# One gather of 8 KB rows for the u and v row of an expert, each pair handled on its own

## The chip, the cores and the metric

One Trainium2 chip; the kernel runs on one of its cores. The metric is the device time of one execution in microseconds (us). The median of three runs of the kernel before is 3246.3 us (3240.91 to 3247.57).

## The reference

Two transformer-like blocks of two layers each, on 256 tokens of width 1024, all in float32. The part that the change touches is the mixture of experts at the end of both layers of the second block. For each token it picks the 128 best of 16384 experts (8 heads with 16 each), with a gate for each. Every expert has a row `u` and a row `v` of 1024 numbers. The result is

```
act = einsum('td,thkd->thk', x, u_tab[idx])        # one dot product per picked expert
wgt = gelu(act) * gate
y   = einsum('thk,thkd->td', wgt, v_tab[idx])      # the weighted sum of the v rows
```

## The kernel before

The kernel is one program of many stages, one after the other on the core. Each stage is a block in which the five engines run their own instruction streams and meet at semaphores.

The experts are computed in two ways side by side. For 192 of the 256 tokens (`DENSE`) all 16384 experts are computed as matrix products, with gates that are zero where an expert was not picked. There are 128 rows of 128 experts (`NK`). For the other 64 tokens (`ROWS_OF`) only the picked experts are used: 64 tokens by 128 picks are 8192 pairs of token and expert, laid on 128 partitions by 64 columns, so that two partitions share a token. For each of the 64 columns an indirect DMA fetches one `u` row per partition, later another fetches one `v` row per partition, 4 KB per partition, 512 KB in all.

`experts_stage` (from line 2637, run from 1729 to about 2285 us and from 2666 us to the end) does both. Its parts:

- SyncE (SP) fetches the matrix tiles: `v` tiles of 512 KB into a ring of four (line 255), `u` tiles of 512 KB (line 2683) into another ring of four.
- PE takes, for each row j of experts, ten matmuls of 128x512 (`combine`, lines 2731 to 2735) and, for all rows from the 35th on, the `u` products of a row two further on (`activate`, line 2718). The first 28 rows (`EARLY`) have had their `u` product in an earlier stage, six more (`MID`) too.
- ACT splits each `v` tile in two float32r parts: it writes the high one (`high`, line 2784), and applies gelu to the `u` products (line 2777).
- DVE writes the low part (`low`, line 2844), weighs the activations with the gates (`weigh`, lines 2834, 2836, 2815), and between these does the work of the 64 other tokens: `dot` (line 2851) multiplies a gathered `u` row with the token and sums it into a column of `row_act`; `add_row` (lines 2859 and 2862) adds a gathered `v` row times its weight to `y_rows`.
- POOL issues the 128 gathers (line 2708) into a ring of six slots of 4 KB (`row_ring`, `ROW_SLOTS`), first all `u` rows, then all `v` rows. Gather n waits until the row that lay in its slot has been used: `pool.wait_ge(row_step, n - ROW_SLOTS + 1)`.

The order is written out by hand: `order` (line 2647) is a list of 228 steps, a v step (`low` of a tile two rows ahead) and a u step (`weigh` of a row two ahead) in turn once the early rows are over. DVE and ACT walk through it in the same order. `dots_at` and `adds_at` (line 2656) say after which steps a dot or an add is put. All 64 dots come at steps 3 to 124, all adds at steps 131 to 227. Between them stands one gelu over all 64 columns on ACT (line 2795) and one multiplication by the gates on DVE (line 2879). DVE may run ahead of PE by two rows at most, since the split ring has two places (`SPLIT`) and the weights two buffers. PE in turn can take a row only when its weights and both its halves are there (`weighted`, `low_ready`).

The same 24 KB per partition that hold the six slots are also the place where the stage before keeps the six `u` tiles of the `MID` rows (line 2304). `y_rows` holds two thirds of their activations until they are weighed. `choose_stage` writes the indices of the rows into `row_at` (line 2519).

Of the kernel before, what the change touches and what calls it, by code (L numbers as in the profile page):

```python
# [72 lines left out]
EARLY = 28  # L73
# [2 lines left out]
DENSE = 192  # L76
ROWS_OF = SEQ - DENSE
PEER = NK * NK
ROW_SLOTS, MID = 6, 6

RAW, SPLIT = 4, 2
SUMS_LATE = 3
# [2183 lines left out]
def choose_stage(k, l, weights, norm, ahead):  # L2266
# [3 lines left out]
    nc, pairs = k.nc, TB * PH  # L2270
# [3 lines left out]
    with stage(nc, *WEIGHT_SEMS, "keys_in", "kept", "scored", "scores_used", "row_step", "step", "gate_step", "turned",  # L2274
# [136 lines left out]
        def _(dve):  # L2411
# [21 lines left out]
            rows = Steps(dve, row_step)  # L2433
# [5 lines left out]
            s = Steps(dve, step)  # L2439
# [73 lines left out]
            own, at, rows = slice(SLOTS, 2 * SLOTS), k.late_at[:, 0:SLOTS], slice(DENSE - P, P)  # L2513
            s(nc.vector.scalar_tensor_tensor(at, k.key_i[:, own], float(NK), k.key_j[:, own], ALU.mult, ALU.add))
            dve.wait_ge(gate_step, 6)
            for half in range(2):
                to, cols = slice(half * ROWS_OF, (half + 1) * ROWS_OF), slice(half * ROWS_OF, (half + 1) * ROWS_OF)
                for which in range(2):
                    nc.vector.tensor_scalar(k.row_at[to, which, :], at[rows, cols], float((2 * l + which) * PEER), None, ALU.add).then_inc(step, 1)
                nc.vector.tensor_copy(k.row_gate[to, :], k.gates[rows, SLOTS + half * ROWS_OF:SLOTS + (half + 1) * ROWS_OF]).then_inc(step, 1)  # L2520
            dve.wait_ge(turned, 1)
            for n, x in enumerate((k.slot_i, k.slot_j, k.slot_gate)):
# [114 lines left out]
def experts_stage(k, l, weights, norm, ahead, out_dram):  # L2637
# [4 lines left out]
    nc, rows = k.nc, NK - EARLY  # L2642
# [9 lines left out]


    sums = ROWS_OF
    places = sorted([*range(3, EARLY, 4), *(t for t in range(EARLY + 2 * MID, len(order)) if is_v[t]), *range(EARLY + 2 * MID + 1, len(order) - 8, 6)])
    dots_at, adds_at = places[:sums], places[-sums:]
    gelu_at, weigh_at = dots_at[-1] + 1, dots_at[-1] + 2
    assert weigh_at < adds_at[0], (weigh_at, adds_at[0])
    row_slot = lambda n: k.row_ring[:, n % ROW_SLOTS, :]
    rows_there = lambda n: 16 * (l * len(range(n % ROW_SLOTS, 2 * sums, ROW_SLOTS)) + n // ROW_SLOTS + 1)  # L2660

    with stage(nc, *WEIGHT_SEMS, "u_in_0", "u_in_1", "u_in_2", "u_in_3", "u_done", "gelu_done", "weight_step", "weighted", "kept_0", "kept_1", "turned", "added", "stored", "ahead_high", "ahead_low",
               "row_step", "row_gelu", "row_weighed", *Norm.SUMS, weights=weights) as (
            block, high_ready, low_ready, halves_used, u_in_0, u_in_1, u_in_2, u_in_3, u_done, gelu_done, weight_step, weighted, kept_0, kept_1, turned, added, stored, ahead_high, ahead_low,
            row_step, row_gelu, row_weighed, squared, sums_done):
        weights.signals(high_ready, low_ready, halves_used)
        u_in = (u_in_0, u_in_1, u_in_2, u_in_3)
        if norm:
# [32 lines left out]

        @block.gpsimd
        def _(pool):
            for n in range(2 * sums):
                if n >= ROW_SLOTS:
                    pool.wait_ge(row_step, n - ROW_SLOTS + 1)
                at = k.row_at[:, n // sums, n % sums:n % sums + 1]
                nc.gpsimd.indirect_dma_start(row_slot(n), None, k.peer_rows, bass.IndirectOffsetOnAxis(ap=at, axis=0)).then_inc(  # L2708
                    k.rows_in[n % ROW_SLOTS], 16)

        @block.tensor
        def _(pe):
# [43 lines left out]
                late_row((rows - MID) // RAW, m)  # L2756
            for j in range(NK - 2, NK):
                combine(j, j % 2, False, j == NK - 1)
            pe.wait_ge(row_step, 2 * sums)
            for m in range(pairs):  # L2760
                pe.wait_ge(kept_0, m // 2 + 1)
                pe.wait_ge(kept_1, m // 2 + 1)
                for c in (2 * m, 2 * m + 1):
                    out, cols = k.ps[:, turned_in[m], c % 2 * SEQ:(c % 2 + 1) * SEQ], slice(c * P, (c + 1) * P)
# [7 lines left out]
        @block.scalar  # L2772
        def _(act):
            def activate(q):
                act.wait_ge(u_done, q - MID + 1)
                act.wait_ge(weighted, q + EARLY + 1)
                nc.scalar.activation(k.gelu[:, q % 2, 0:DENSE], k.ps[:, q % 2, 0:DENSE], ACT.Gelu_apprx_tanh).then_inc(gelu_done, 1)  # L2777

            def high(j):

                act.wait_ge(weights.loaded[j % RAW], 16 * (j // RAW + 1))
                for half, cols in enumerate(weights.halves):
                    act.wait_ge(halves_used, v_used(j - SPLIT) + half - 1)
                    nc.scalar.activation(weights.split[:, weights.half_slot(j), 0, cols], weights.ring[:, weights.slot(j), cols], ACT.Copy).then_inc(high_ready, 1)  # L2784

            act.sem_inc(gelu_done, 2)
            weights.high_given(act)
            for t, (v, n) in enumerate(order):
                if v and n + SPLIT < NK:
                    high(n + SPLIT)  # L2790
                if not v and n >= MID:
                    activate(n)
                if t == gelu_at:
                    act.wait_ge(row_step, sums)
                    nc.scalar.activation(k.row_act[:, :], k.row_act[:, :], ACT.Gelu_apprx_tanh).then_inc(row_gelu, 1)
            if norm:
                ahead.high_ahead(act, 0, weights.left(NK - 2))
            act.wait_ge(halves_used, v_used(NK - 1))
            for half in range(2):
                nc.scalar.activation(k.y_natural[:, 0, half * 512:(half + 1) * 512], outs[half], ACT.Copy).then_inc(kept_0, 1)  # L2800
            if norm:
                norm.warm(act)
            for m in range(pairs if norm else 0):
                act.wait_ge(added, m + 1)
                nc.scalar.activation(norm.squares[:, 2 * m:2 * m + 2, :], k.x2T[:, 2 * m:2 * m + 2, :], ACT.Square).then_inc(squared, 2)
            if norm:
                ahead.high_ahead(act, 1, weights.left(NK - 1))

        @block.vector
        def _(dve):  # L2810
# [36 lines left out]
            def dot(n):  # L2847


                dve.wait_ge(k.rows_in[n % ROW_SLOTS], rows_there(n))  # L2850
                nc.vector.tensor_tensor_reduce(row_slot(n), row_slot(n), k.x_rows, 1.0, 0.0, ALU.mult, ALU.add,  # L2851
                                               k.row_act[:, n:n + 1]).then_inc(row_step, 1)

            def add_row(n):
                w = k.row_weight[:, n - sums:n - sums + 1]
                dve.wait_ge(k.rows_in[n % ROW_SLOTS], rows_there(n))
                if n == sums:
                    dve.wait_ge(row_weighed, 1)
# [9 lines left out]
            for t, (v, n) in enumerate(order):  # L2868
                if v and n + SPLIT < NK:
                    low(n + SPLIT)  # L2870
                if t + SPLIT < EARLY:
                    split_early(t + SPLIT)
                if not v:
                    weigh(n)
                for n in [n for n, at in enumerate(dots_at) if at == t]:
                    dot(n)
                if t == weigh_at:
                    dve.wait_ge(row_gelu, 1)
                    nc.vector.tensor_tensor(k.row_weight[:, :], k.row_act[:, :], k.row_gate[:, :], ALU.mult).then_inc(row_weighed, 1)
                for n in [n for n, at in enumerate(adds_at) if at == t]:  # L2880
                    add_row(sums + n)
            if norm:
                ahead.low_ahead(dve, 0, 0)
            dve.wait_ge(halves_used, v_used(NK - 1))
# [10 lines left out]
def second_block(k, scope, sb, out):  # L2895

    nc = k.nc
# [8 lines left out]
    k.hot_i, k.hot_j = hot(16, NK), hot(16, NK)  # L2906
    gates = sb(scope, "gates", SEQ * NK)
    k.pair, k.h2F = sb(scope, "pair", ROWS_OF), sb(scope, "h2F", DC, SEQ)
    k.row_at = sb(scope, "row_at", 2, ROWS_OF, dtype=U32)
    k.row_gate, k.row_act, k.row_weight = (sb(scope, f"row_{n}", ROWS_OF) for n in ("gate", "act", "weight"))  # L2910
    tail = Carver(gates[:, DENSE * NK:])
    k.early = gates[:, 0:EARLY * DENSE].rearrange("p (j t) -> p j t", j=EARLY)
    k.dense = gates[:, EARLY * DENSE:DENSE * NK]
    k.u_ring = gates[:, 0:RAW * D].rearrange("p (s m) -> p s m", s=RAW)
    k.x_rows, k.y_rows, k.row_ring = tail(D), tail(D), tail(ROW_SLOTS, D)


    mix = Carver(gates)
# [44 lines left out]
def layout2(x):  # L2963
# [23 lines left out]
    return {  # L2987
        "small2_dram": small2, "w_mixing": mixing.reshape(L * MIX_TILES, P, D), "w_choose": np.concatenate([query, pu[:, :EARLY]], axis=1).reshape(-1, P, D),
        "peer_keys": x["peer_keys"].transpose(0, 4, 1, 2, 3).reshape(L, P, HC * NK),
        "peer_u": pu[:, EARLY:].reshape(-1, P, D), "peer_v": pv.reshape(-1, P, D), "peer_rows": np.stack([x["peer_u"], x["peer_v"]], axis=1).reshape(-1, D),  # L2990
    }


# [229 lines left out]
```

## Time and profile before

| what | us |
|---|---|
| median of three runs | 3246.3 |
| profiled execution, its own time | 3233.7 |
| its span, first to last instruction | 3231.9 |
| first experts stage, from its first gather to its last add | 1730 to 2285 |
| second experts stage | 2666 to 3232 |

Busy time of an engine is the time in which it worked on an instruction, waiting left out; a busy share near 1 in a stretch says that this engine sets its pace. The columns of a windows view are: stretch, its length, busy us of PE, of its weight loads (PEld), of DVE, ACT and POOL, each with the number of instructions, then the granted clock of TensorE (1.00 is 2.4 GHz, 0.50 is 1.2 GHz), the mean busy share of the 16 DMA engines and the GB/s that they moved. In a timeline, times in square brackets are idle time before the instruction, with what ended it.

### The profile page before, as it was taken

How to read it: one execution, taken by the hardware profiler on the slowest of the kernel's cores; microseconds unless marked ns; L12 is line 12 of the kernel's file. 1: busy time of each engine (PE TensorE's matmuls, PEld its weight loads, DVE VectorE, ACT ScalarE, POOL GpSimd, SP SyncE). 2: the span in 40 equal slices, each digit the busy share in tenths (PEclk: the TensorE clock that was granted, in tenths of full speed). 3: DMA queues.
4: the chain of work that ended last, by engine and by line, in shares of the span. 5: the costliest groups of instructions: out<-in, count | busy, mean ns of one | idle time of the engine just before them, and what ended most of it. 6: DMA issues, size and time to landing. Idle time of an engine off the chain costs nothing. (4 is left out here: it accounts for less than half of the span.)

```text
span 3231.9 us, 52114 instructions
## 1 busy us (share of the span) xinstructions
PE 3097.7 (96%) x17744; PEld 2679.3 (83%) x17744; DVE 2371.6 (73%) x4997; ACT 1403.3 (43%) x2729; POOL 632.0 (20%) x556
## 2 busy tenths in 40 slices
PE   7899999999999999899999999999999998999999
PEld 5767776777867999888987799999789986899998
DVE  5667776776666677565978788788656887887887
ACT  5454333332336665475356333333465274333332
POOL 0000000000000000064434132222356061222221
PEclk9999999999999999899999999999999999999999
DMA  6115533434322545433545799999434518899996
GB/s 222 43 59 183 176 144 113 154 124 158 110 71 87 174 156 168 148 121 115 170 130 210 274 354 356 328 356 356 159 101 140 183 50 318 313 353 339 343 357 249
DMA packets 176414, 643.50 MB, mean 199 GB/s; under 512 B 20352, under 2 KB 20736, under 8 KB 175360
## 3 DMA queue, kind: packets, MB, share of 16 engines
q1 hardware_dynamic: 138672, 504.62, 45.0%
q0 software_dynamic: 36864, 134.23, 11.3%
q10 hardware_dynamic: 720, 2.71, 0.2%
q8 instruction: 78, 1.28, 0.2%
q14 instruction: 80, 0.66, 0.1%
HBM read 640.44 MB, written 1.05 MB: 198 GB/s over the span
## 5 line engine op out<-in xcount | busy, mean ns | idle before, releaser
L338 ACT ACTIVATE split<-ring 128x512 fp32r<-128x512 f32 (+1 forms) x644 | 397.6, 624 | 699.4 <-PE ps L224 666.5
L224 PE MATMUL ps<-hT,split 128*128 128x512 f32 (+1 forms) x3504 | 631.1, 341 | 6.5 <-DVEq L322 3.4
L224 PEld LDWEIGHTS ps<-hT,split 128*128 128x128 f32 x3504 | 546.5, 191 | 91.3 <-DVE hT L593 9.7
L347 POOL TENSOR_TENSOR split<-ring,split 128x512 fp32r<-128x512 f32 x184 | 244.3, 1338 | 1528.3 <-ACT split L338 1523.7
L2718 PE MATMUL ps<-h2F,gates 128*128 128x192 f32 x3008 | 519.2, 326 | 0.0
L347 DVE TENSOR_TENSOR split<-ring,split 128x512 fp32r<-128x512 f32 (+1 forms) x460 | 307.2, 678 | 283.3 <-ACT split L338 282.4
L2718 PEld LDWEIGHTS ps<-h2F,gates 128*128 128x128 f32 x3008 | 498.4, 190 | 17.1
L2784 ACT ACTIVATE split<-ring 128x512 fp32r<-128x512 f32 x504 | 317.4, 632 | 358.3 <-PE ps L2735 333.6
L2844 DVE TENSOR_TENSOR split<-ring,split 128x512 fp32r<-128x512 f32 x504 | 340.1, 689 | 118.0 <-ACT split L2784 115.4
L2708 POOL DMA_INDIRECT gates<-peer_rows,row_at x256 | 267.7, 1046 | 809.9 <-DVE row_act L2851 462.9
L2731 PE MATMUL ps<-split,chunk 128*128 128x512 f32 x512 | 232.1, 453 | 16.9 <-DVE chunk L2815 16.3
L2777 ACT ACTIVATE gelu<-ps 128x192 f32<-128x192 f32 x188 | 62.1, 330 | 370.2 <-PE ps L2718 370.2
L224 PE MATMUL ps<-h2T,split 128*128 128x256 f32 x1632 | 209.1, 285 | 4.3 <-DVE gates L2147 3.5
L224 PEld LDWEIGHTS ps<-h2T,split 128*128 128x128 f32 x1632 | 199.1, 191 | 11.8 <-DVE h2T L591 5.4
L2733 PE MATMUL ps<-split,chunk 128*128 128x512 f32 x512 | 203.6, 398 | 0.0
L2734 PE MATMUL ps<-split,chunk 128*128 128x512 f32 x512 | 203.4, 397 | 0.0
L2735 PE MATMUL ps<-split,chunk 128*128 128x512 f32 x512 | 203.2, 397 | 0.0
L2732 PE MATMUL ps<-split,chunk 128*128 128x512 f32 x512 | 202.7, 396 | 0.0
L224 PE MATMUL ps<-act_chunk,split 128*128 128x512 f32 (+1 forms) x1056 | 191.9, 343 | 0.0
L224 PEld LDWEIGHTS ps<-act_chunk,split 128*128 128x128 f32 x1056 | 164.2, 192 | 25.0 <-issue 0.6
L2862 DVE SCALAR_TENSOR_TENSOR gates<-gates,row_weight 128x1024 f32<-128x1024 f32 x126 | 161.0, 1278 | 0.2
L2851 DVE CUSTOM_DVE_ANT_0 gates<-gates 128x1024 f32<-128x1024 f32 x128 | 155.9, 1218 | 0.0
(394 smaller groups left out, 4758.2 us busy)
## 6 DMA issues: line engine op xcount, KB each, us to landing
ring<-peer_v SPq DMA_DIRECT2D x256, 512.0 KB
gates<-peer_u SPq DMA_DIRECT2D x200, 512.0 KB, 6.9
ring<-w_up SPq DMA_DIRECT2D x88, 512.0 KB, 3.8
ring<-w_choose SPq DMA_DIRECT2D x88, 512.0 KB, 3.5
ring<-w_mixing SPq DMA_DIRECT2D x68, 512.0 KB, 3.6
ring<-w_merge SPq DMA_DIRECT2D x64, 512.0 KB, 4.1
ring<-w_down SPq DMA_DIRECT2D x44, 512.0 KB, 3.7
mix_row_ring<-w_mod SPq DMA_DIRECT2D x40, 512.0 KB, 3.7
```

The source lines that it names most:

```text
L224: ins = nc.tensor.matmul(out, lhsT(a), rhs(b), start=first and n == 0, stop=last and n == len(PASSES) - 1)
L338: self.nc.scalar.activation(self.split[:, self.half_slot(s), 0, cols], self.ring[:, self.slot(s), cols], ACT.Copy).then_inc(self.high_read ...
L347: (ops or self.nc.vector).tensor_tensor(self.split[:, self.half_slot(s), 1, cols], self.ring[:, self.slot(s), cols], self.split[:, self.ha ...
L2708: nc.gpsimd.indirect_dma_start(row_slot(n), None, k.peer_rows, bass.IndirectOffsetOnAxis(ap=at, axis=0)).then_inc(k.rows_in[n % ROW_SLOTS] ...
L2718: last = nc.tensor.matmul(k.ps[:, m % 2, 0:DENSE], k.u_ring[:, m % RAW, c * P:(c + 1) * P], k.h2F[:, c, 0:DENSE], start=c == 0, stop=c == ...
L2731: nc.tensor.matmul(outs[half], high, v(0), start=first, stop=False)
L2732: nc.tensor.matmul(outs[2 + half], pair, v(0), start=first, stop=False)
L2733: nc.tensor.matmul(outs[half], low, v(0), start=False, stop=False)
L2734: nc.tensor.matmul(outs[2 + half], pair, v(1), start=False, stop=last)
L2735: ins = nc.tensor.matmul(outs[half], high, v(1), start=False, stop=last)
L2784: nc.scalar.activation(weights.split[:, weights.half_slot(j), 0, cols], weights.ring[:, weights.slot(j), cols], ACT.Copy).then_inc(high_re ...
L2844: nc.vector.tensor_tensor(weights.split[:, weights.half_slot(j), 1, cols], weights.ring[:, weights.slot(j), cols], weights.split[:, weight ...
```

## The change

The table of rows in memory is laid out anew: the `u` and `v` row of an expert lie side by side in one row of 8 KB. One gather fetches both. The ring has three slots of 8 KB in the same place. The column n of picks is then dotted, activated, weighed and added for itself. The gather of column n + 3 waits for the add of column n. Gelu and the multiplication with the gate are done on ACT, on one column of 128x1, at the step after each dot. New lists say when: the first three dots at steps 3, 11 and 19, the first add at step 40, then an add and a dot in turn, each at the next of the listed places.

```diff
-ROW_SLOTS, MID = 6, 6
+ROW_SLOTS, MID = 3, 6
...
-                for which in range(2):
-                    nc.vector.tensor_scalar(k.row_at[to, which, :], at[rows, cols], float((2 * l + which) * PEER), None, ALU.add).then_inc(step, 1)
+                nc.vector.tensor_scalar(k.row_at[to, :], at[rows, cols], float(l * PEER), None, ALU.add).then_inc(step, 1)
...
-    places = sorted([*range(3, EARLY, 4), *(t for t in range(EARLY + 2 * MID, len(order)) if is_v[t]), *range(EARLY + 2 * MID + 1, len(order) - 8, 6)])
-    dots_at, adds_at = places[:sums], places[-sums:]
-    gelu_at, weigh_at = dots_at[-1] + 1, dots_at[-1] + 2
+    places = sorted([*range(3, EARLY, 4), *(t for t in range(EARLY + 2 * MID, len(order)) if is_v[t]), *range(EARLY + 2 * MID + 1, len(order) - 8, 4)])
+    places = [*places[:2 * ROW_SLOTS:2], *[t for t in places if t > order.index((False, MID - 1))]]
+    places = [places[n * len(places) // (2 * sums)] for n in range(2 * sums)]
+    dots_at = [*places[:ROW_SLOTS], *places[ROW_SLOTS + 1:2 * sums - 1:2]][:sums]
+    adds_at = [*places[ROW_SLOTS:2 * sums - ROW_SLOTS:2], *places[2 * sums - ROW_SLOTS:2 * sums]]
+    adds_at = adds_at[-sums:]
+    gelu_at = {at + 1: n for n, at in enumerate(dots_at)}
...
-            for n in range(2 * sums):
+            for n in range(sums):
                 if n >= ROW_SLOTS:
-                    pool.wait_ge(row_step, n - ROW_SLOTS + 1)
-                at = k.row_at[:, n // sums, n % sums:n % sums + 1]
-                nc.gpsimd.indirect_dma_start(row_slot(n), None, k.peer_rows, bass.IndirectOffsetOnAxis(ap=at, axis=0)).then_inc(
+                    pool.wait_ge(row_added, n - ROW_SLOTS + 1)
+                at = k.row_at[:, n:n + 1]
+                nc.gpsimd.indirect_dma_start(pair_of(n), None, k.peer_rows, bass.IndirectOffsetOnAxis(ap=at, axis=0)).then_inc(
...
+            def weigh_row(n):
+                w = k.row_weight[:, n:n + 1]
+                act.wait_ge(row_step, n + 1)
+                nc.scalar.activation(w, k.row_act[:, n:n + 1], ACT.Gelu_apprx_tanh).then_inc(row_gelu, 1)
+                act.wait_ge(row_gelu, n + 1)
+                nc.scalar.activation(w, w, ACT.Copy, scale=k.row_gate[:, n:n + 1]).then_inc(row_weighed, 1)
...
-                if t == gelu_at:
-                    act.wait_ge(row_step, sums)
-                    nc.scalar.activation(k.row_act[:, :], k.row_act[:, :], ACT.Gelu_apprx_tanh).then_inc(row_gelu, 1)
+                if t in gelu_at:
+                    weigh_row(gelu_at[t])
...
             def add_row(n):
-                w = k.row_weight[:, n - sums:n - sums + 1]
-                dve.wait_ge(k.rows_in[n % ROW_SLOTS], rows_there(n))
+                w = k.row_weight[:, n:n + 1]
+                dve.wait_ge(row_weighed, n + 1)
...
-                if t == weigh_at:
-                    dve.wait_ge(row_gelu, 1)
-                    nc.vector.tensor_tensor(k.row_weight[:, :], k.row_act[:, :], k.row_gate[:, :], ALU.mult).then_inc(row_weighed, 1)
...
-"peer_rows": np.stack([x["peer_u"], x["peer_v"]], axis=1).reshape(-1, D)
+"peer_rows": np.stack([x["peer_u"], x["peer_v"]], axis=2).reshape(-1, 2 * D)
```

At the end of the stage PE waits for the 64th add (`row_added`) where it waited for the 128th step of `row_step`.

## Rows read from the trace of the kernel before

**Rows 1.** The page: busy us of each engine, and the granted clock in slices.
```profile
PE 3097.7 (96%) x17744; PEld 2679.3 (83%) x17744; DVE 2371.6 (73%) x4997; ACT 1403.3 (43%) x2729; POOL 632.0 (20%) x556
...
PEclk9999999999999999899999999999999999999999
```

**Rows 2.** Windows over the first experts stage (columns as told above).
```profile
1730.00:1820.00 90.00, 81.98 (x327) 61.30 (x327) 71.73 (x180) 39.82 (x64) 14.01 (x13) 0.96 0.85 303
1820.00:2055.00 235.00, 235.00 (x1244) 213.73 (x1243) 188.36 (x405) 76.38 (x144) 61.23 (x58) 1.00 0.93 340
2055.00:2275.00 220.00, 220.00 (x1161) 199.84 (x1160) 184.39 (x328) 71.76 (x135) 58.72 (x57) 1.00 0.94 348
```

**Rows 3.** Waits, 2060 to 2270 us: total us, times, longest.
```profile
POOL gates L2708 <- DVE gates L2862: 143.9, 54, 4.0
...
DVE split L2844 <- ACT split L2784: 17.8, 56, 0.4
DVE gated L2834 <- ACT gelu L2777: 11.9, 29, 0.4
```

**Rows 4.** Timeline of PE: the same matmul in two rows, start and length.
```profile
1936.76 0.53 PE L2731 MATMUL ps<-split,chunk 128*128 128x512 f32 x1
...
1941.68 0.53 PE L2731 MATMUL ps<-split,chunk 128*128 128x512 f32 x1
```

**Rows 5.** Groups by line, 1820 to 2275 us; L2519 by itself.
```profile
L2862 DVE SCALAR_TENSOR_TENSOR gates<-gates,row_weight 128x1024 f32<-128x1024 f32 x59 | 75.4, 1278 | 0.0
L2851 DVE CUSTOM_DVE_ANT_0 gates<-gates 128x1024 f32<-128x1024 f32 x57 | 69.4, 1217 | 0.0
...
L2851 DVE DVE_READ_ACCUMULATOR2_ANT row_act<- 128x1 f32 x57 | 4.6, 81 | 0.0
...
L2879 DVE TENSOR_TENSOR row_weight<-row_act,row_gate 128x64 f32<-128x64 f32 x1 | 0.2, 218 | 0.0
...
L2795 ACT ACTIVATE row_act<-row_act 128x64 f32<-128x64 f32 x1 | 0.2, 249 | 0.0
...
L2519 DVE TENSOR_SCALAR row_at<-gates x8: 186/190/193, 1652.3 to 2589.8; 64x64 uint32<-64x64 f32 x8
```

**Rows 6.** Timeline of DVE, 2156 to 2161 us: lows, add, weighing.
```profile
2156.68 1.28 DVE L2844 TENSOR_TENSOR split<-ring,split 128x512 fp32r<-128x512 f32 x2
2157.88 1.27 DVE L2862 SCALAR_TENSOR_TENSOR gates<-gates,row_weight 128x1024 f32<-128x1024 f32 x1
2159.15 0.51 DVE L2834 TENSOR_TENSOR gated<-gelu,gates 128x192 f32<-128x192 f32 x1
...
2160.67 0.69 DVE L2844 TENSOR_TENSOR split<-ring,split 128x512 fp32r<-128x512 f32 x1 [0.26 <-ACT split L2784]
```

**Rows 7.** DMA issues by line: size, median us from issue to landing.
```profile
gates<-peer_u SPq DMA_DIRECT2D x200, 512.0 KB, 6.9
...
gates<-peer_keys SPq DMA_DIRECT2D x2, 1024.0 KB, 4.8
```

**Rows 8.** The gathers, the last at 3199.1 us, and windows after it.
```profile
L2708 POOL DMA_INDIRECT gates<-peer_rows,row_at x256: 933/1042/1912, 1729.9 to 3199.1; - x128
...
3199.00:3202.00 3.00, 3.00 (x17) 2.68 (x16) 2.25 (x6) 1.26 (x2) 1.04 (x1) 1.00 0.88 322
3202.00:3205.00 3.00, 3.00 (x17) 2.66 (x16) 2.50 (x6) 0.76 (x2) 0.00 (x0) 1.00 0.90 358
3205.00:3208.00 3.00, 3.00 (x20) 2.89 (x18) 2.35 (x3) 0.83 (x2) 0.00 (x0) 1.00 0.07 30
```

**Rows 9.** One window of 1 us at the start of the stage.
```profile
1732.00:1733.00 1.00, 1.00 (x6) 0.82 (x5) 0.00 (x0) 0.45 (x1) 0.69 (x2) 1.00 1.03 422
```

**Rows 10.** PE over its longest gap: timeline, then windows.
```profile
1805.99 0.80 PE L2731 MATMUL ps<-split,chunk 128*128 128x512 f32 x1 [3.75 <-DVE chunk L2815]
...
1803.00:1804.00 1.00, 0.00 (x0) 0.00 (x0) 1.00 (x2) 0.00 (x0) 0.00 (x0) 1.00 0.67 221
1805.00:1811.00 6.00, 5.00 (x12) 3.94 (x13) 2.76 (x9) 0.96 (x2) 0.96 (x1) 0.50 0.53 173
```

More of the change, by code:

```diff
@@ L2654, in experts_stage @@
     sums = ROWS_OF
-    places = sorted([*range(3, EARLY, 4), *(t for t in range(EARLY + 2 * MID, len(order)) if is_v[t]), *range(EARLY + 2 * MID + 1, len(order) - 8, 6)])
-    dots_at, adds_at = places[:sums], places[-sums:]
-    gelu_at, weigh_at = dots_at[-1] + 1, dots_at[-1] + 2
-    assert weigh_at < adds_at[0], (weigh_at, adds_at[0])
-    row_slot = lambda n: k.row_ring[:, n % ROW_SLOTS, :]
-    rows_there = lambda n: 16 * (l * len(range(n % ROW_SLOTS, 2 * sums, ROW_SLOTS)) + n // ROW_SLOTS + 1)
+    places = sorted([*range(3, EARLY, 4), *(t for t in range(EARLY + 2 * MID, len(order)) if is_v[t]), *range(EARLY + 2 * MID + 1, len(order) - 8, 4)])
+    places = [*places[:2 * ROW_SLOTS:2], *[t for t in places if t > order.index((False, MID - 1))]]
+    assert len(places) >= 2 * sums, len(places)
+    places = [places[n * len(places) // (2 * sums)] for n in range(2 * sums)]
[3 more added lines that the diff above has]
+    gelu_at = {at + 1: n for n, at in enumerate(dots_at)}
+    assert len(adds_at) == sums and all(dots_at[n] > adds_at[n - ROW_SLOTS] for n in range(ROW_SLOTS, sums))
+    assert len(gelu_at) == sums
+    pair_of = lambda n: k.pair_ring[:, n % ROW_SLOTS, :]
+    row_slot = lambda n, which: k.pair_ring[:, n % ROW_SLOTS, which * D:(which + 1) * D]
+    rows_there = lambda n: 16 * (l * len(range(n % ROW_SLOTS, sums, ROW_SLOTS)) + n // ROW_SLOTS + 1)
     with stage(nc, *WEIGHT_SEMS, "u_in_0", "u_in_1", "u_in_2", "u_in_3", "u_done", "gelu_done", "weight_step", "weighted", "kept_0", "kept_1", "turned", "added", "stored", "ahead_high", "ahead_low",
-               "row_step", "row_gelu", "row_weighed", *Norm.SUMS, weights=weights) as (
+               "row_step", "row_gelu", "row_weighed", "row_added", *Norm.SUMS, weights=weights) as (
             block, high_ready, low_ready, halves_used, u_in_0, u_in_1, u_in_2, u_in_3, u_done, gelu_done, weight_step, weighted, kept_0, kept_1, turned, added, stored, ahead_high, ahead_low,
-            row_step, row_gelu, row_weighed, squared, sums_done):
+            row_step, row_gelu, row_weighed, row_added, squared, sums_done):
         weights.signals(high_ready, low_ready, halves_used)
@@ L2758, in _ @@
                 combine(j, j % 2, False, j == NK - 1)
-            pe.wait_ge(row_step, 2 * sums)
+            pe.wait_ge(row_added, sums)
             for m in range(pairs):
@@ L2850, in dot @@
                 dve.wait_ge(k.rows_in[n % ROW_SLOTS], rows_there(n))
-                nc.vector.tensor_tensor_reduce(row_slot(n), row_slot(n), k.x_rows, 1.0, 0.0, ALU.mult, ALU.add,
+                u = row_slot(n, 0)
+                nc.vector.tensor_tensor_reduce(u, u, k.x_rows, 1.0, 0.0, ALU.mult, ALU.add,
                                                k.row_act[:, n:n + 1]).then_inc(row_step, 1)
             def add_row(n):
-                w = k.row_weight[:, n - sums:n - sums + 1]
-                dve.wait_ge(k.rows_in[n % ROW_SLOTS], rows_there(n))
-                if n == sums:
-                    dve.wait_ge(row_weighed, 1)
-                    nc.vector.tensor_scalar(k.y_rows, row_slot(n), w, None, ALU.mult).then_inc(row_step, 1)
-                else:
-                    dve.wait_ge(row_step, n)
-                    nc.vector.scalar_tensor_tensor(k.y_rows, row_slot(n), w, k.y_rows, ALU.mult, ALU.add).then_inc(row_step, 1)
+                w = k.row_weight[:, n:n + 1]
+                dve.wait_ge(row_weighed, n + 1)
+                if n == 0:
+                    nc.vector.tensor_scalar(k.y_rows, row_slot(n, 1), w, None, ALU.mult).then_inc(row_added, 1)
+                else:
+                    dve.wait_ge(row_added, n)
+                    nc.vector.scalar_tensor_tensor(k.y_rows, row_slot(n, 1), w, k.y_rows, ALU.mult, ALU.add).then_inc(row_added, 1)
             dve.sem_inc(weighted, 2)
@@ L2876, in _ @@
                     dot(n)
-                if t == weigh_at:
-                    dve.wait_ge(row_gelu, 1)
-                    nc.vector.tensor_tensor(k.row_weight[:, :], k.row_act[:, :], k.row_gate[:, :], ALU.mult).then_inc(row_weighed, 1)
                 for n in [n for n, at in enumerate(adds_at) if at == t]:
-                    add_row(sums + n)
+                    add_row(n)
             if norm:
@@ L2908, in second_block @@
     k.pair, k.h2F = sb(scope, "pair", ROWS_OF), sb(scope, "h2F", DC, SEQ)
-    k.row_at = sb(scope, "row_at", 2, ROWS_OF, dtype=U32)
+    k.row_at = sb(scope, "row_at", ROWS_OF, dtype=U32)
     k.row_gate, k.row_act, k.row_weight = (sb(scope, f"row_{n}", ROWS_OF) for n in ("gate", "act", "weight"))
@@ L2914, in second_block @@
     k.u_ring = gates[:, 0:RAW * D].rearrange("p (s m) -> p s m", s=RAW)
-    k.x_rows, k.y_rows, k.row_ring = tail(D), tail(D), tail(ROW_SLOTS, D)
+    k.x_rows, k.y_rows, k.pair_ring = tail(D), tail(D), tail(ROW_SLOTS, 2 * D)
+    k.row_ring = k.pair_ring.rearrange("p s (n m) -> p (s n) m", n=2)
     mix = Carver(gates)
@@ L2989, in layout2 @@
         "peer_keys": x["peer_keys"].transpose(0, 4, 1, 2, 3).reshape(L, P, HC * NK),
-        "peer_u": pu[:, EARLY:].reshape(-1, P, D), "peer_v": pv.reshape(-1, P, D), "peer_rows": np.stack([x["peer_u"], x["peer_v"]], axis=1).reshape(-1, D),
+        "peer_u": pu[:, EARLY:].reshape(-1, P, D), "peer_v": pv.reshape(-1, P, D), "peer_rows": np.stack([x["peer_u"], x["peer_v"]], axis=2).reshape(-1, 2 * D),
     }
```

## The prediction

> **What bounds the kernel now.** I read the page first, for which engine fills the span. PE is busy 96% of it, DVE 73%, and the granted clock is full almost everywhere [rows 1]. An average over stages does not say what an experts stage waits for, so I cut the first one in windows. From 1820 to 2275 us PE is busy for every microsecond (235.00 of 235, 220.00 of 220), at clock 1.00. DVE stands at 188.4 of 235 and 184.4 of 220, the DMA engines at 0.93 to 0.94 with 340 to 348 GB/s [rows 2]. PE sets the pace; DVE has some 16 to 20% to spare. The waits say the same from the other side: DVE waits for ACT and ACT for PE, in short pieces of at most 0.4 us, and nobody on DVE waits for a gather. Only POOL waits long, for adds to free a slot (143.9 us in 54 waits), which costs nothing there [rows 3]. The timeline gives the price of a row of experts: the same matmul comes again after 1941.68 - 1936.76 = 4.92 us [rows 4]. A row is one v and one u step of the list, so a step takes 2.46 us at PE's pace.
>
> **The change, part by part.** The bytes stay: 64 gathers of 1 MB for 128 of 512 KB. The dots and adds stay too, 64 each per stage. What moves is when a slot comes free. Before, slot n was free after a dot or an add six uses back, so a gather had some nine steps to land. Now the two rows of a pair share a slot, and it is held from the dot until the add, because the gather of pair n + 3 waits for add n. I worked out the two lists from the diff. Add n stands at steps 40, 42, 45, 49 ..., dot n + 3 at steps 41, 44, 46, 50 .... From the first add (40) to dot 63 (220) there are 61 such pairs of places and 180 steps. 90 steps lie between an add and the dot that needs its slot (36 times one step, 21 times two, 4 times three) and 90 between that dot and the next add. The dot-to-add distance is 6 to 8 steps, in which the slot only waits. So the gather is asked to come in 1 to 3 steps, and DVE, which runs in order, stands still at the dot until it lands. Behind the dot queue the low parts and the weighings on which PE's next rows depend.
>
> The **cycle of DVE per pair** is then: gather (G), dot, 1.5 steps, add. With the pieces taken where DVE runs back to back: a dot 1.22 [rows 5], an add 2159.15 - 2157.88 = 1.27, a v step 2157.88 - 2156.68 = 1.20, a u step 2160.67 - 2159.15 - 0.26 = 1.26, so 1.23 for a mean step [rows 6]. That makes 1.22 + 1.5 x 1.23 + 1.27 = 4.3 us beside G. The 1.5 steps after an add run beneath the gather. PE needs 180 / 61 = 2.95 steps x 2.46 = 7.3 us per pair. So DVE becomes the bound as soon as G is over 7.3 - 4.3 = 3.0 us.
>
> **How long is G?** No gather of 1 MB is in the trace, so I bound it. From below: a plain transfer of 1 MB (128 rows of 8 KB) lands 4.8 us after its issue [rows 7], and a gather should not be quicker, since the POOL instruction itself lasts 1.04 [rows 8]. From above: 512 KB tiles fetched in a burst land in 6.9 us [rows 7]; the last gather of 512 KB, issued at 3199.1 with a v tile, a u tile and another gather under way, had DMA traffic behind it until between 3205 and 3208, so 6 to 9 us [rows 8]. At 422 GB/s, the highest rate that the engines show [rows 9], 1.05 MB takes 2.5 of the 4.8 us, which leaves 2.3 us fixed. If the gather got only a third of the 350 GB/s of the full stage, G would be 2.3 + 9.0 = 11.3 us. But a slower stage fetches its tiles more slowly: 1.5 rows of 1.05 MB per cycle of about 11 us are 140 GB/s. Between the steady 350 and the peak of 422 I take 385; 245 are left for the gather, so 1.05 MB takes 4.3 us and G is 6.6 us. That is nearer to the quiet row than to the crowded ones, as the queues are emptier than before.
>
> The Trainium skill has a fit for this path ("DMA: Bandwidth & Descriptors", "Anatomy of one DMA — SWDGE (gpsimd) path"): some 2.0 us plus the bytes at 436 GB/s. Its estimate is 4.4 us for 1 MB against 3.2 for 512 KB, which speaks for one large gather and still leaves DVE waiting; the sum would be about 3440 us by it.
>
> **ACT.** Two activations of 128x1 come after each dot; the nearest row is the 128x64 gelu of 0.249 us [rows 5], so 0.5 us a pair, 32 us a stage on an engine busy a third of it [rows 2]. ACT now waits for the dot, with the high part of the next v tile and the next gelu behind it. The dot is what DVE waits at too, so both are released together; DVE has one step (1.23) of work before it needs ACT again. Between nothing and 0.5 us a pair I take 0.25. The weights themselves are ready 5 steps before the add.
>
> **Small ones.** Four dots fewer stand in the early rows (steps 7 to 27 had six, now two), 4 x 1.22 = 4.9 us of DVE. There PE is busy 82 of 90 us and DVE 72 [rows 2], so part of it shows. The dot at step 27 stood right before the weighing that ended a gap of 3.75 us and a time at clock 0.50 [rows 10]; without it perhaps 3 us more come back. From 0 to 8 us a stage, I take 5. Two of four index writes of 0.19 us go, and one multiplication of 0.22 [rows 5]: under 1 us.
>
> **The sum.** Stretch from add 0 to dot 63 in one stage: 61 x (6.6 + 0.25) + 61 x 1.22 + 60 x 1.27 + 90 x 1.23 = 418 + 74 + 76 + 111 = 679 us. At PE's pace it was 180 x 2.46 = 443. So +236 a stage, +472 in two, less 10 early: +462 on the profiled execution's 3233.7, which gives 3696. That execution lies 12.6 us under the median of the runs (3246.3); with them, 3708, and I say 3705. With G = 4.8 and no ACT term it is 3233.7 + 2 x (293 + 261 - 443) - 16 + 12.6 = 3452; with 11.3, 2 x (705 + 261 - 443) more than before: about 4290.
>
> **The rivals.**
> - Clock. PE would idle some 4 us in each cycle of 11. The one gap of that size now, 3.75 us, is followed by at least 6 us at 0.50, and the matmuls take longer in it [rows 10]. 6 us at half rate cost 3 us of PE work: 7.3 + 3 = 10.3 per pair, just beneath the cycle, so in the forecast it hides. If gelu results come late by it and DVE waits again, a cycle grows by up to 3 us: 122 x 3 = 366 more, 4070; half of it, 3890, is the likelier size. The Trainium skill ("TensorE: Matmul & The Clock Gate", "HAM oscillation — how this bites in real kernels") tells of just this, bursts of matmuls between DMA waits that each start at the low clock.
> - The gather lands near its quiet time, 4.8 to 5.3 us: 3450 to 3520. The rows of 8 KB may move faster than two of 4 KB, and the tiles may be done before each gather starts.
> - Faster. The gather fits in the 3.0 us of cover, PE stays the bound and only the early dots count: 3246 - 10 = 3236. It decides at G = 3.0. Moving the bytes takes 2.5 us even alone [rows 9], and nothing of this size landed under 4.8 [rows 7].
> - Nothing happens: DVE's lead of two rows, 9.8 us, swallows the waits. It would swallow one, not 61 in a row, each of which is 4 us longer than PE's 7.3. Or the lists keep fewer gathers waiting than I read: 3246.
>
> **How the numbers follow.** Forecast 0.70, clock 0.15, near-quiet gather 0.09, faster 0.03, nothing 0.03. The range leaves out the two last, the far half of the clock's case and G over 8.7: 3500 to 3960. Slower by over 0.2% (about what a measurement here tells from no change) 0.94, within 0.03, faster 0.03.
>
> **What would show it.** DVE's longest wait becomes the dot, for the gather, 61 times a stage, about 3 to 5 us each, some 500 us in all; POOL's wait for the add stays. PE idles a third of the stage with DVE as releaser, busy near 65%. DMA falls from 345 GB/s to about 230, in the first 90 us from 303 to about 260. The stage from 1820 us grows by some 235 us. I am wrong if the dots do not wait, if the second wait is ACT's for the dot with DVE's behind ACT, or if the clock stays at 0.50 and DVE waits for gelu.

## The result, and the profile after

The changed kernel takes 3724.2 us (median of six runs, 3711.97 to 3736.59), the kernel before 3249.2 us in the same runs. The ratio is 1.1455, 95% interval 1.1422 to 1.1487: 14.6% slower. The forecast was 3705 us with 3500 to 3960 around it.

The page of the changed kernel, its first parts:

```profile
PE 3254.0 (88%) x17744; PEld 2777.7 (75%) x17744; DVE 2341.8 (63%) x4991; ACT 1424.9 (38%) x2983; POOL 495.2 (13%) x428
...
PEclk9999999999999989999988888889999998898888
...
q0 software_dynamic: 18432, 134.23, 9.7%
```

Against [rows 1] PE fell from 96% to 88% of the span and DVE from 73% to 63%, though neither has less work (DVE 2341.8 us for 2371.6): it is waiting that came in. PE's busy time even grew by 156 us without one matmul more. The clock row says why: it stands at 8 to 9 tenths in the experts stages, so the same matmuls last longer.

Windows over the first experts stage, the same stretches as in [rows 2]:

```profile
1730.00:1820.00 90.00, 82.31 (x339) 61.04 (x338) 69.54 (x180) 42.58 (x74) 3.06 (x3) 1.00 0.78 264
1820.00:2055.00 235.00, 181.90 (x822) 157.74 (x821) 120.60 (x247) 52.77 (x135) 20.38 (x20) 0.86 0.61 226
2055.00:2275.00 220.00, 166.90 (x749) 144.77 (x749) 113.97 (x231) 49.24 (x124) 20.28 (x20) 0.87 0.64 234
```

Where PE was busy 235.00 of 235 us it is now 181.90, and DVE 120.60 for 188.36. The DMA engines fell from 340 to 226 GB/s. No engine is full any more, so a chain of waits sets the pace. The waits of 2060 to 2270 us, to be held against [rows 3], name its links:

```profile
POOL gates L2714 <- DVE gates L2874: 184.6, 18, 11.3
ACT row_weight L2795 <- DVE row_act L2864: 125.5, 19, 9.3
DVE gates L2864 <- DMA gates<-peer_rows,row_at: 101.4, 19, 6.8
...
PE ps L2737 <- DVE chunk L2827: 53.1, 17, 5.9
...
DVE split L2856 <- ACT split L2790: 0.4, 1, 0.4
```

DVE waits for a gather at 19 dots of this stretch, 101.4 us, where before it never did. PE waits for DVE's weights behind it, ACT for the dot, and POOL for the add. DVE itself waits for ACT once, 0.4 us. Over the whole kernel the wait at the dot is 633.5 us in 122 times:

```profile
DVE gates L2864 <- DMA gates<-peer_rows,row_at: 633.5, 122, 8.1
```

122 is 2 x 61, every dot but the first three of each stage. The timeline of DVE shows one cycle:

```profile
2042.36 1.28 DVE L2874 SCALAR_TENSOR_TENSOR gates<-gates,row_weight 128x1024 f32<-128x1024 f32 x1
2043.56 0.50 DVE L2846 TENSOR_TENSOR gated<-gelu,gates 128x192 f32<-128x192 f32 x1
...
2044.39 0.43 DVE L2827 TENSOR_TENSOR chunk<-gated,chunk 128x64 fp32r<-128x64 f32 x2
2050.73 1.23 DVE L2864 CUSTOM_DVE_ANT_0 gates<-gates 128x1024 f32<-128x1024 f32 x1 [5.91 <-DMA gates<-peer_rows,row_at]
...
2055.47 1.28 DVE L2874 SCALAR_TENSOR_TENSOR gates<-gates,row_weight 128x1024 f32<-128x1024 f32 x1
```

The add ends at 2043.64, one weighing follows, then 5.91 us of nothing until the pair is there at 2050.73. From dot to the next add there is no wait. Over all pairs, from the start and end times of these instructions, 7.09 us lie between the end of an add and the start of the dot that needs its slot (6.5 to 7.6 for 8 in 10), 2.95 from that dot's start to the start of the next add, and a cycle is 11.32 us. The stretch from add 0 to dot 63 is 686.9 us in the first stage and 686.5 in the second.

Taken apart by the start times of each row's first matmul, in us, both experts stages:

| | before | after |
|---|---|---|
| rows 0 to 28 | 76.0 + 76.6 | 74.4 + 73.8 |
| rows 28 to 34 | 22.4 + 21.9 | 20.3 + 21.4 |
| rows 34 to 127 | 455.7 + 455.7 | 695.7 + 695.9 |
| all else in the span | 2123.5 | 2128.6 |

The late rows lost 480.2 us, rows 0 to 34 gave back 7.0, and the rest is 5 us, less than what that part differs by from run to run (2118 to 2154 us over all the runs below).

### The profile page after: what moved, and what is told of

The parts are those of the page before. It is cut to its first block and busy times, and to the rows that moved or that the text cites. A ratio compares the mean times of both kernels' runs of the same rounds, so it can differ in the third digit from the quotient of the medians.

```text
span 3710.2 us, 52233 instructions
## 1 busy us (share of the span) xinstructions
PE 3254.0 (88%) x17744; PEld 2777.7 (75%) x17744; DVE 2341.8 (63%) x4991; ACT 1424.9 (38%) x2983; POOL 495.2 (13%) x428
## 3 DMA queue, kind: packets, MB, share of 16 engines
q0 software_dynamic: 18432, 134.23, 9.7%
HBM read 640.44 MB, written 1.05 MB: 173 GB/s over the span
## 5 line engine op out<-in xcount | busy, mean ns | idle before, releaser
L2864 DVE CUSTOM_DVE_ANT_0 gates<-gates 128x1024 f32<-128x1024 f32 x128 | 156.8, 1225 | 633.5 <-DMA gates<-peer_rows,row_at 633.5
L2737 PE MATMUL ps<-split,chunk 128*128 128x512 f32 x512 | 254.8, 498 | 339.5 <-DVE chunk L2827 339.3
L2724 PEld LDWEIGHTS ps<-h2F,gates 128*128 128x128 f32 x3008 | 524.5, 198 | 21.6
L2724 PE MATMUL ps<-h2F,gates 128*128 128x192 f32 x3008 | 539.0, 334 | 0.0
L2737 PEld LDWEIGHTS ps<-split,chunk 128*128 128x128 f32 x512 | 108.8, 213 | 402.9 <-issue 359.0
L2790 ACT ACTIVATE split<-ring 128x512 fp32r<-128x512 f32 x504 | 302.0, 624 | 263.1 <-PE ps L2741 240.1
L2856 DVE TENSOR_TENSOR split<-ring,split 128x512 fp32r<-128x512 f32 x504 | 330.1, 686 | 52.4 <-ACT split L2790 52.2
L2795 ACT ACTIVATE row_weight<-row_act 128x1 f32<-128x1 f32 x128 | 25.9, 203 | 840.1 <-DVE row_act L2864 839.8
L2714 POOL DMA_INDIRECT gates<-peer_rows,row_at x128 | 130.6, 1021 | 1430.8 <-DVE gates L2874 1225.7
L2738 PE MATMUL ps<-split,chunk 128*128 128x512 f32 x512 | 228.2, 446 | 0.0
L2739 PE MATMUL ps<-split,chunk 128*128 128x512 f32 x512 | 228.0, 445 | 0.0
L2740 PE MATMUL ps<-split,chunk 128*128 128x512 f32 x512 | 227.0, 443 | 0.0
L2741 PE MATMUL ps<-split,chunk 128*128 128x512 f32 x512 | 226.2, 442 | 0.0
```

The costliest lines, as they stand in the source:

```text
L2724: last = nc.tensor.matmul(k.ps[:, m % 2, 0:DENSE], k.u_ring[:, m % RAW, c * P:(c + 1) * P], k.h2F[:, c, 0:DENSE], start=c == 0, stop=c == ...
L2737: nc.tensor.matmul(outs[half], high, v(0), start=first, stop=False)
L2738: nc.tensor.matmul(outs[2 + half], pair, v(0), start=first, stop=False)
L2739: nc.tensor.matmul(outs[half], low, v(0), start=False, stop=False)
L2740: nc.tensor.matmul(outs[2 + half], pair, v(1), start=False, stop=last)
L2741: ins = nc.tensor.matmul(outs[half], high, v(1), start=False, stop=last)
```

## The experiments

The theory: a gather of 1 MB stands between an add and the next dot on DVE's in-order path, so each of 61 cycles per stage lasts its latency and 4.2 us of DVE work more. Rivals: PE at its low clock sets the pace; the pair-by-pair work (small activations on ACT, dots and adds in turn) costs; the 8 KB rows move badly.

The runs a1, a2, a3 and c1 leave out work or data and were executed once each; their differences are read inside the traces, from the stretch from add 0 to dot 63 and the late rows, which agree between the two stages of a run within a few us.

### a1 and a2: is PE the bound?

```diff
-                    nc.tensor.matmul(outs[half], low, v(0), start=False, stop=False)
```

a1, on the changed kernel:

> The changed kernel with one of the ten matmuls of combine left out per half row (the product of the low part of the weights), so 8 instead of 10 per row of experts; part of the sum is left out. PE's row falls from 4.92 us by 2 x 0.23 to 4.46 us. Theory (the gather between add and dot stands on DVE's path, PE has room): the stretch from add 0 to dot 63 stays at 687 us a stage, the cycle at 11.3 us, and only the rows outside it gain, so 3724 less 0 to 25. Rival (PE at the low clock sets the pace): 0.46 us at full clock or 0.93 at half over 90 rows and two stages, 80 to 165 us less.

a2, on the kernel before:

> The kernel before with the same matmuls left out; part of the sum is left out. PE sets its pace there, so 94 rows x 0.465 us x 2 stages = 87 us less in the late rows and 0 to 10 in the early ones: 3249 - 87 to 97, some 3155. DVE works about 4.1 us a row, less than 4.46, so PE stays the bound. If DVE or the transfers (344 GB/s already) were the next bound close by, clearly less than 87 would come.

a2 took 3141.4 us, 92 less than the profiled execution before (3233.7). Its late rows went from 455.7 to 412.3 us a stage, 87 us in two, as expected of PE's share. a1 took 3690.8 us, 33 under the changed kernel's median, where 0 to 25 were expected. Its span is 21 us under that of the changed kernel's profiled execution, of which 13 are in rows 0 to 34 and 7 in the later ones; the stretch from add 0 to dot 63 hardly moved (681.9 and 685.5 us for 686.9 and 686.5). Windows of a1 and then of the changed kernel:

```profile
2060.00:2480.00 420.00, 299.75 (x1332) 261.57 (x1333) 221.72 (x450) 93.99 (x243) 39.31 (x38) 0.86 0.64 236
```

```profile
2060.00:2480.00 420.00, 317.23 (x1429) 274.97 (x1427) 216.65 (x438) 92.50 (x237) 38.33 (x37) 0.88 0.63 232
```

PE works 299.75 instead of 317.23 us of the same 420 at about the same clock, and the stretch gets shorter by 5 us at most. The same cut is worth 43 us of late rows per stage where PE is the bound and up to 5 where the gather is. The rival of the clock falls: the low clock is real (0.86 to 0.88 in these windows), but nearly all of its cost lies in time in which PE would wait.

### a3 and c1: what the 7.1 us are made of

```diff
-                nc.gpsimd.indirect_dma_start(pair_of(n), None, k.peer_rows, bass.IndirectOffsetOnAxis(ap=at, axis=0)).then_inc(
+                nc.gpsimd.indirect_dma_start(pair_of(n)[:, 0:D], None, k.peer_rows, bass.IndirectOffsetOnAxis(ap=at, axis=0)).then_inc(
...
-"peer_rows": np.stack([x["peer_u"], x["peer_v"]], axis=2).reshape(-1, 2 * D)
+"peer_rows": x["peer_u"].reshape(-1, D)
```

> The changed kernel, but each gather fetches only the u row (4 KB per partition, 512 KB), the lists and waits stay; the v rows are left out, the adds take what lies there. Theory: of the 7.1 us from the end of an add to the dot, 2.3 are fixed and 4.8 are transfer; half the bytes give some 4.7 to 5.2 us, a cycle of 9.1, and 2 x 61 x 2.1 = 256 us less: about 3465. If nearly all of it were fixed cost of a gather: over 3620. If the clock or ACT set the pace instead of the gather: nearly 3724.

It took 3530.1 us, 194 less. Per pair, 5.53 us were left from add to dot, 1.56 less, not 2.1. So the second 512 KB are worth 1.56 us, 336 GB/s. That alone does not tell what the other 5.53 us are. c1 keeps the gather whole and takes the other traffic away:

```diff
-                sp.dma_start(k.u_ring[:, q % RAW, :], tile(k.peer_u, l * rows + MID + q)).then_inc(u_in[q % RAW], 16)
+                sp.dma_start(k.u_ring[:, q % RAW, 0:64], tile(k.peer_u, l * rows + MID + q)[:, 0:64]).then_inc(u_in[q % RAW], 16)
...
-                weights.fetch(sp, j // RAW, j % RAW)
+                sp.dma_start(weights.ring[:, weights.slot(j % RAW), 0:64], tile(weights.dram, weights.base + j)[:, 0:64]).then_inc(weights.loaded[j % RAW], 16)
```

> The changed kernel with its gathers of 1 MB as they are, but of each v and u tile that the experts stage itself fetches only 64 of 1024 columns (32 KB instead of 512); the rest of each tile is left out, so the output is not the reference's. Measures the gather with the DMA engines nearly to itself. In the changed kernel 7.1 us pass from the end of an add to the start of the dot. Theory (the v and u tile asked for just before the add move at the same time, 2.1 MB together at about 390 GB/s): without them 1.05 MB less at 390 GB/s, 2.7 us off each, so 4.4 us, a cycle of 8.6 and 2 x 61 x 2.7 = 330 us less: about 3395. Rival (tiles spread evenly over the cycle, 139 GB/s of 385, fixed part 2.3 us as the forecast had it): 2.3 + 2.7 = 5.0 us, 3470. If G is mostly a fixed time: 6.5 us or more, over 3650.

It took 3573.0 us. All three figures of the expectation missed: 5.87 us remain, 1.2 less than with the tiles. The gather's own timeline in c1, then windows of 1 us after its issue at 2000.85, then the dot:

```profile
2000.85 0.97 POOL L2714 DMA_INDIRECT gates<-peer_rows,row_at  x1 [10.69 <-DVE gates L2874]
```

```profile
2001.00:2002.00 1.00, 1.00 (x8) 1.00 (x7) 0.69 (x3) 0.58 (x1) 0.82 (x1) 1.00 0.07 15
2002.00:2003.00 1.00, 1.00 (x8) 1.00 (x7) 0.00 (x0) 0.00 (x0) 0.00 (x0) 1.00 0.63 131
2003.00:2004.00 1.00, 1.00 (x7) 0.92 (x6) 0.00 (x0) 0.00 (x0) 0.00 (x0) 1.00 0.94 344
2004.00:2005.00 1.00, 1.00 (x6) 0.77 (x6) 0.00 (x0) 0.00 (x0) 0.00 (x0) 1.00 0.93 393
2005.00:2006.00 1.00, 1.00 (x6) 0.86 (x5) 0.00 (x0) 0.00 (x0) 0.00 (x0) 1.00 0.45 180
```

```profile
2006.20 1.23 DVE L2864 CUSTOM_DVE_ANT_0 gates<-gates 128x1024 f32<-128x1024 f32 x1 [4.45 <-DMA gates<-peer_rows,row_at]
```

The add ended at 2000.58. The data begin between 2002 and 2003 and fill 131 + 344 + 393 + 180 GB/s times 1 us, the 1.05 MB of the pair, in under 4 us. Windows of 0.2 us give their ends:

```profile
2002.20:2002.40 0.20, 0.20 (x4) 0.20 (x3) 0.00 (x0) 0.00 (x0) 0.00 (x0) 1.00 0.00 0
2002.40:2002.60 0.20, 0.20 (x3) 0.20 (x3) 0.00 (x0) 0.00 (x0) 0.00 (x0) 1.00 1.32 287
...
2005.40:2005.60 0.20, 0.20 (x2) 0.15 (x2) 0.00 (x0) 0.00 (x0) 0.00 (x0) 1.00 0.31 123
2005.60:2005.80 0.20, 0.20 (x3) 0.15 (x2) 0.00 (x0) 0.00 (x0) 0.00 (x0) 1.00 0.01 0
```

Over all 122 pairs of c1, from the times of the gather's own packets in the trace, the 5.87 us are 0.28 from the end of the add to the issue, 1.72 from there to the first packet, 3.48 of data and 0.38 from the last packet to the dot. So 2.4 us pass without the gather's data, and 3.5 with them, at a mean of 301 GB/s. In the changed kernel the same windows carry two things:

```profile
2044.50:2045.50 1.00, 1.00 (x4) 0.81 (x3) 0.32 (x2) 0.07 (x1) 0.39 (x1) 0.50 0.99 389
2045.50:2046.50 1.00, 1.00 (x5) 0.91 (x4) 0.00 (x0) 0.49 (x1) 0.00 (x0) 0.50 1.03 401
2046.50:2047.50 1.00, 1.00 (x6) 1.00 (x4) 0.00 (x0) 0.14 (x1) 0.00 (x0) 0.60 1.10 410
2047.50:2048.50 1.00, 1.00 (x8) 1.00 (x8) 0.00 (x0) 0.00 (x0) 0.00 (x0) 1.00 0.95 352
2048.50:2049.50 1.00, 1.00 (x7) 0.96 (x7) 0.00 (x0) 0.00 (x0) 0.00 (x0) 1.00 0.74 311
```

```profile
2042.47 0.33 SPq L255 DMA_DIRECT2D ring<-peer_v  x1
2042.84 0.43 SPq L2689 DMA_DIRECT2D gates<-peer_u  x1
```

A v and a u tile were issued 1.4 us before the gather (2043.91), because SP's fetch waits for the low part that DVE writes just ahead of the add. In this cycle the packets of the tiles run until 2046.93 and those of the gather from 2046.63 to 2050.34: the engines carry 389 to 410 GB/s, but the tiles go first. Over all pairs of the changed kernel the 7.09 us are 0.28 to the issue, 2.36 to the first packet, 4.03 of data (260 GB/s) and 0.42 to the dot. So 7.1 us = 2.4 without data + 3.5 for the pair + 1.2 for the tiles in its way, of which 0.7 come as a later start and end and 0.5 as slower data. In a3 the gather's data take 2.49 us, 1.54 less than here, which is nearly all of its 1.56.

### a4: undo the merging alone

```diff
+            def gather(n, which):
+                at = k.row_at[:, which, n:n + 1]
+                nc.gpsimd.indirect_dma_start(row_slot(n, which), None, k.peer_rows, bass.IndirectOffsetOnAxis(ap=at, axis=0)).then_inc(
+                    k.rows_in[which * ROW_SLOTS + n % ROW_SLOTS], 16)
...
+            for at, which, n in events:
+                if n + ROW_SLOTS < sums:
+                    pool.wait_ge(row_added if which else row_step, n + 1)
+                    gather(n + ROW_SLOTS, which)
```

`events` are the dots and adds in the order of their steps. With the gathers the table of rows and the two sets of indices of before come back, and an add waits for its own `v` row.

> The changed kernel with its lists, its gelu and weighing pair by pair, but u and v row in gathers of their own again: the u row of pair n+3 is fetched after dot n, the v row after add n. Nothing else moves. Theory (what costs is that the u half is held until the add): a u gather gets 7 to 8 steps, no wait of DVE for a gather, PE's pace again: 3225 to 3250. Rival (the pair-by-pair work on ACT, or the alternation of dots and adds on DVE, costs): it stays over 3400.

3238.1 us, ratio 0.9954 (0.9927 to 0.9981) to the kernel before. The late rows take 455.7 us a stage again, with the lists, the alternation and the small activations of the change all in place. The rival of the pair-by-pair work falls, and with it a cost of ACT of any such size. What costs 480 us in this order is that the u half of a slot cannot be refilled between its dot and the add of its v half.

### b1 and b2: keep the merging, change the order

```diff
-    dots_at = [*places[:ROW_SLOTS], *places[ROW_SLOTS + 1:2 * sums - 1:2]][:sums]
-    adds_at = [*places[ROW_SLOTS:2 * sums - ROW_SLOTS:2], *places[2 * sums - ROW_SLOTS:2 * sums]]
-    adds_at = adds_at[-sums:]
+    dots_at, adds_at, lead = [*places[:ROW_SLOTS]], [], 2
+    for at in places[ROW_SLOTS:]:
+        ahead_of = len(adds_at) - (len(dots_at) - ROW_SLOTS)
+        if len(dots_at) < sums and ahead_of >= lead:
+            dots_at.append(at)
+        else:
+            adds_at.append(at)
```

> The changed kernel with another order on the same places: add n+1 stands before dot n+3 (the add of a pair comes 3 places after its dot and not 5, the dot that needs its slot 3 places after the add and not 1). Theory: the cover for the gather grows from 3.0 by one pair's time of 7.3 to 10.3 us. A gather of 1 MB at the full load of the stage needs 7 to 11 us, so most dots do not wait, some do: 3235 to 3290. Rival (pair-by-pair work costs, not the gather): over 3400.

b1 took 3250.3 us, ratio 0.9997 (0.9974 to 1.0019). Its dots waited ten times, 13.7 us in all, the late rows took 457.4 and 457.3 us:

```profile
L2718 POOL DMA_INDIRECT gates<-peer_rows,row_at x128: 936/1100/1827, 1744.6 to 3218.2; - x128
...
  DVE gates L2868: 13.7, 10
...
DMA to landing us min/median/max: 5.6/7.7/14.6
```

So at the full load of 355 GB/s a gather of 1 MB lands in 7.7 us at the median. The 14.6 belong to the start of a stage, where three gathers are issued at once (9.3, 12.0 and 14.5 us in the first stage); all others land within 9.9. b2 has `lead = 3`:

> The same, two pairs: the add comes on the next place after its dot, the dot that needs its slot 5 places after the add, so the cover is 17.5 us. Theory: no dot waits for a gather, PE is busy throughout from 1840 us on, and the early rows keep their gain of 5 us a stage: 3235 to 3245, 0.1 to 0.4% under the kernel before. A new wait could be the add for ACT's weight, one step after the dot: up to 0.5 us a pair, hidden beneath PE's pace.

b2 took 3240.8 us, ratio 0.9973 (0.9949 to 0.9997), late rows 455.7 us, no dot waiting. With covers of 3.0, 10.3 and 17.5 us and nothing else changed, the late rows take 696, 457 and 456 us. Both runs keep the gathers of 8 KB rows, so the rival that these rows move badly falls too.

### b3: the early dots alone

```diff
-    places = sorted([*range(3, EARLY, 4), *(t for t in range(EARLY + 2 * MID, len(order)) if is_v[t]), *range(EARLY + 2 * MID + 1, len(order) - 8, 6)])
+    places = sorted([*range(3, EARLY - 4, 8), *(t for t in range(EARLY + 2 * MID, len(order)) if is_v[t]), *range(EARLY + 2 * MID + 1, len(order) - 8, 5)])
```

> The kernel before with three dots in the early rows (steps 3, 11, 19) instead of seven, the rest later; nothing else changed. It measures the one gain that the forecast had: 5 us a stage, so 10 us or 0.3% less (3239). Rival: the early rows wait for ACT and the transfers anyway, no difference within 0.2%.

3246.9 us, ratio 0.9991 (0.9967 to 1.0016): the interval holds both. Inside the profile, where other stages don't blur it, rows 0 to 28 took 73.2 and 74.2 us for 76.0 and 76.6, so 2.6 us a stage, half of the 5.

### c2, d1 and d2: no work for the other tokens in the early rows

```diff
-    places = [*places[:2 * ROW_SLOTS:2], *[t for t in places if t > order.index((False, MID - 1))]]
+    places = [t for t in places if t > order.index((False, MID - 1))]
```

> The kernel with u and v rows in gathers of their own (the run a4), and in addition no dot before step 38, so that the 28 early rows have none of the other tokens' work on DVE. Theory: the first 28 rows took 76.0 us with seven dots, 73.5 with three; each dot less gives 0.6 us, so some 72 us and 3 us for the whole kernel, 0.1% under a4. Against the kernel before 0.3 to 0.5% less. Rival: the early rows are at PE's and ACT's pace already, nothing changes against a4.

> The change's own gathers of 8 KB rows, with the order of b2 (add on the next place after its dot, 17.5 us of cover) and no dot before step 38. Theory: no dot waits for a gather, the late rows stay at 455.7 us a stage, the early ones fall to some 71 us as in c2: the same time as d2 within 0.2%, 0.3 to 0.6% under the kernel before. Rival: the gathers of 1 MB, now all in the late rows, come too late for some dots again: 1 to 5 us a stage over d2.

> The same kernel as c2, beside d1 on one chip. The same as d1 within 0.2%; 0.3 to 0.6% under the kernel before.

c2 took 3234.2 us, ratio 0.9942 (0.9919 to 0.9964); on another chip, as d2, 3238.8, ratio 0.9969 (0.9945 to 0.9994). d1 took 3238.1, ratio 0.9971 (0.9948 to 0.9993). Rows 0 to 28 take 70.8 and 71.5 us in c2, 72.0 and 72.7 in d1, late rows 455.7 in both. Windows of the early rows of the kernel before and of c2:

```profile
1760.00:1780.00 20.00, 18.97 (x80) 14.28 (x79) 17.31 (x44) 9.94 (x16) 2.29 (x2) 1.00 0.87 288
```

```profile
1760.00:1780.00 20.00, 20.00 (x85) 15.05 (x84) 16.43 (x44) 10.62 (x18) 0.00 (x0) 1.00 0.81 258
```

PE went from 18.97 of 20 us to 20.00. Rows 0 to 28 are 5.2 and 5.1 us shorter in c2 and 4.0 and 3.9 in d1, 8 to 10 us in two stages, 0.3%. d1 and d2 measured that as a whole (0.3%), c2 more (0.6%, interval 0.36 to 0.81), which the early rows alone do not explain. Merged gathers and separate ones cannot be told apart once the order gives them time.

## Why the prediction was right

- **The bound of before and where a slot comes free.** Right. a2 shows PE's pace, the dots waited 122 times as counted from the lists, and a4 and b2 show that freeing the slot in time takes the whole loss away.
- **The DVE pieces beside the gather.** 4.3 us forecast; 11.32 - 7.09 = 4.23 measured.
- **The gather.** 6.6 us forecast, 7.09 measured. The transfer was costed at 4.3 us and took 4.03. The fixed part was costed at 2.3 us, from a plain load of 1 MB; the time without the gather's data is 3.06 us in the changed kernel and 2.38 in c1. The forecast had no term for the 0.28 us from the add to the issue, nor for tiles that go first: it spread them evenly over the cycle, where SP issues a pair of them just before the gather. So 0.76 us were missing and 0.27 were too much. That the share of 245 GB/s came near the measured mean of 260 is luck: the tiles take the first part of the time and leave the engines to the gather afterwards (the second 512 KB moved at 336 GB/s, as a3 showed). The upper bound of 11.3 us was far off (8.7 at most from issue to landing, the first three of a stage left out). That 512 KB tiles took 6.9 us in [rows 7] told of a queue of six, not of a single one.
- **ACT.** 0.25 us a pair forecast, nothing measured: from dot to add 2.95 us, under the 3.07 of the pieces alone. The two activations are 0.2 and 0.3 us long, about what [rows 5] had. The term was a guess between two bounds, and it happens to cover half of what G lacked.
- **The early rows.** 10 us forecast, 7.0 measured over rows 0 to 34. The gap of 3.75 us of [rows 10] shrank to 2.61 in the first stage, and no half-clock time followed it there; but the dots themselves were worth 2.6 us a stage only, as b3 showed.
- **The sum.** 679 us for the stretch, 687 measured; 472 - 10 forecast, 480 - 7 measured, plus 5 elsewhere in the span.
- **The clock's case.** Its premise came true in part (0.86 in the stage), its price did not: a1 shows that PE's time was not the bound. The forecast had reckoned 7.3 + 3 = 10.3 us of PE work, beneath the cycle, for a low-clock time in each cycle. In the first stage the clock fell to 0.50 only 30 times in 61 cycles, so PE works 8.7 us per cycle of 11.3 (520.94 of 680 us from 1840 to 2520) and has more room than reckoned.
- **What the text asked the profile to show.** The dot waits came as said, somewhat longer (5.2 us each, 633 in all, for "3 to 5" and "some 500"). DMA fell to 226 to 234 GB/s ("about 230"). PE stands at 76% busy, not 65%, since the low clock stretched its matmuls. One sign of being wrong came halfway: ACT's wait for the dot is the second on the list (125.5 us from 2060 to 2270), longer than DVE's for the gather. But DVE waits behind ACT for 0.4 us only, so ACT is held up by the dot and holds nobody up.
- **The figure of the Trainium skill.** The fit of the Trainium skill ("DMA: Bandwidth & Descriptors", "Anatomy of one DMA — SWDGE (gpsimd) path") gives an estimate of 4.4 us for 1 MB. From issue to landing c1 measured 5.5 us at the median, with the engines nearly idle, and the changed kernel 6.9. The measurement decides: here the fit was short by 1.1 us even on quiet engines.

## What to carry to other kernels

When two transfers are merged, ask when each half of the buffer comes free: the merged slot is free only when the last half is, and the refill then has only the time from there to the next first use. Add up the cycle of the engine that stands in between (latency plus its own work per item) and hold it against the pace of the bound; here 11.3 against 7.3 us. Before giving the merging up, look at the order, since the same merged gathers cost nothing once each add stood next to its dot.

## What the runs showed that was not expected

- One gather of 1 MB takes 5.5 us at the median from issue to landing with the DMA engines nearly idle (c1), 6.9 in the changed kernel, and 7.7 at the full load of 355 GB/s (b1, b2). The load adds less than the forecast's upper bound of 11.3 us had allowed for.
- Rows of 8 KB do not move faster than rows of 4 KB here. The gathers' packets took 11.3% of a span of 3231.9 us before, 365 us of all engines, and 9.7% of 3710.2 us after, 360 us, for the same 134.23 MB (q0 in part 3 of the page). The changed kernel's engines are less loaded; at the same full load b2 with 8 KB rows has 11.2% of 3253.8 us and a4 with 4 KB rows 11.3% of 3236.3, 364 and 366 us.
- A low granted clock may cost next to nothing: PE has 156 us more busy time, yet in a1 a cut of PE's work shortened the stretch by 5.0 and 1.0 us only. No run had the changed kernel at the full clock, so the rest is inferred from a1.
- Fixing what the change had meant to do gave nothing over two separate gathers. Inside the traces the only gain over the kernel before lies in the early rows, from less DVE work there: some 2.6 us a stage with three dots, 4 to 5 with none. The times of whole runs do not order these versions: with three early dots b3 is at 0.9991, b2 at 0.9973 and a4 at 0.9954, with none d2, d1 and c2 at 0.9969, 0.9971 and 0.9942.
